# Closing norm of a block of rows run beside the next block's attention: where its squares, roots and row scaling are issued

## What is computed

```
h  = rmsnorm(x) ; proj = h @ w_in -> q, k, v of A, q and latent of B, indexer, two gates
oA = windowed attention (8 heads, sinks, keys of this and the previous chunk)
oB = attention of 8 heads over the 256 keys that the indexer selects per row
x  = x + (sig(gA) * (oA @ wa) + sig(gB) * (oB @ wb)) @ w_out
x  = x + (silu(rmsnorm(x) @ wg) * (rmsnorm(x) @ wu)) @ wd
out = x * rsqrt(mean(x*x) + eps) * g_f          # the norm that the change moves
```

## Time and profile before

| | us |
|---|---|
| median of 3 runs | 3491.55 (3490.05 to 3493.18) |
| profiled execution, its own time | 3493.45 |
| its span, first to last instruction | 3491.6 |
| PE busy | 3371.6 (97%) |
| DVE, ACT, POOL busy | 1931.6, 1392.0, 1639.3 |
| mean granted TensorE clock | 0.99 |

### The profile page before, as it was taken

The page is one execution under the profiler, slowest core; times in us unless marked ns, Lnnn a source line. Parts: engine busy times, 40 slices in busy tenths (PEclk is TensorE's granted clock), DMA queues, the critical chain, the costliest instruction groups (busy, mean ns, idle before and its releaser), DMA issues.

```text
span 3491.6 us, 44043 instructions
## 1 busy us (share of the span) xinstructions
PE 3371.6 (97%) x16616; PEld 2782.9 (80%) x16616; DVE 1931.6 (55%) x3341; ACT 1392.0 (40%) x2547; POOL 1639.3 (47%) x997
## 2 busy tenths in 40 slices
PE   8999999999999999999999998999999999999998
PEld 6778878788887888788788777977887799778887
DVE  3236657468465655376686627767787378521112
ACT  3224435345534431264454226735552377320001
POOL 4555555444235666402566651045667410256665
PEclk9999999999999999999999999999999999999999
DMA  5745454445342333403333351052333500232332
GB/s 143 205 131 169 112 168 127 123 141 157 126 142 93 93 97 97 162 25 129 109 97 91 96 170 37 1 191 83 97 92 97 181 22 2 84 110 91 96 100 93
DMA packets 420642, 382.34 MB, mean 110 GB/s; under 512 B 19248, under 2 KB 347184, under 8 KB 419792
## 3 DMA queue, kind: packets, MB, share of 16 engines
q1 hardware_dynamic: 396512, 337.16, 31.7%
q10 hardware_dynamic: 23920, 42.36, 3.5%
HBM read 316.68 MB, written 62.78 MB: 109 GB/s over the span
## 4 chain that ended last, share of the span: by engine, by line
PE 88%; DVE 5%; ACT 4%; issue 2%; POOL 1%; ACTq 0%; DMA 0%; SPq 0%; DVEq 0%; POOLq 0%
PE BANK L696 20%; PE BANK L697 20%; PE BANK L698 20%; PE BANK L912 3%; PE LP L696 3%; PE LP L697 3%; PE LP L698 3%; PE BANK L925 2%; PE BANK L927 2%; PE LP L889 2%; PE LP L890 2%; PE LP L788 2%; PE LP L787 2%; PE BANK L936 1%; PE LP L895 1%
## 5 line engine op out<-in xcount | busy, mean ns | idle before, releaser
L666 POOL TENSOR_TENSOR WLO<-WRAW,WHI 128x1024 fp32r<-128x1024 f32 x456 | 1118.4, 2453 | 38.0
L664 POOL TENSOR_SCALAR WHI<-WRAW 128x1024 fp32r<-128x1024 f32 x456 | 505.6, 1109 | 1301.9 <-PE BANK L698 954.2
L696 PE MATMUL BANK<-H2hi,WHI 128*128 128x512 f32 x1408 | 560.7, 398 | 6.7 <-DVE X L1780 4.7
L697 PE MATMUL BANK<-H2lo,WHI 128*128 128x512 f32 x1408 | 558.4, 397 | 0.0
L698 PE MATMUL BANK<-H2hi,WLO 128*128 128x512 f32 x1408 | 558.2, 396 | 0.0
L696 PE MATMUL BANK<-HThi,WHI 128*128 128x512 f32 (+1 forms) x1024 | 408.6, 399 | 2.3 <-DVE QS L1428 2.3
L697 PE MATMUL BANK<-HTlo,WHI 128*128 128x512 f32 (+1 forms) x1024 | 404.9, 395 | 0.0
L698 PE MATMUL BANK<-HThi,WLO 128*128 128x512 f32 (+1 forms) x1024 | 404.6, 395 | 0.0
L1192 ACT ACTIVATE MASK<-SCD,THR 128x896 bf16<-128x896 f32 (+5 forms) x186 | 282.0, 1517 | 221.6 <-DVE THR L1487 195.1
L1817 DVE TENSOR_TENSOR BANK<-BANK,SL 128x512 f32<-128x512 f32 x88 | 61.6, 700 | 477.6 <-PE BANK L698 457.8
L696 PEld LDWEIGHTS BANK<-H2hi,WHI 128*128 128x128 f32 x1408 | 265.5, 189 | 72.4 <-DVE X L1780 5.2
(11 more groups left out here) (245 smaller groups left out, 6528.3 us busy)
## 6 DMA issues: line engine op xcount, KB each, us to landing
WRAW<-in_w_in SPq DMA_DIRECT2D x124, 512.0 KB, 4.4
WRAW<-in_w_ffn_gate SPq DMA_DIRECT2D x88, 512.0 KB, 3.9
WRAW<-in_w_ffn_up SPq DMA_DIRECT2D x88, 512.0 KB, 3.8
WRAW<-in_w_ffn_down SPq DMA_DIRECT2D x88, 512.0 KB, 3.8
qsp<-QS SPq DMA_DIRECT2D x32, 512.0 KB, 5.6
gates<-GS ACTq DMA_DIRECT2D x64, 256.0 KB, 2.2
GL<-gates ACTq DMA_DIRECT2D x64, 256.0 KB, 3.7
WRAW<-in_w_out SPq DMA_DIRECT2D x32, 512.0 KB, 4.3
```

What stands on the lines that cost most here:

```text
L664: nc.gpsimd.tensor_scalar(hi, raw, 1.0, 1.0, ALU.mult, ALU.mult).then_inc(w_hi, 1)
L666: nc.gpsimd.tensor_tensor(lo, raw, hi.bitcast(f32), ALU.subtract).then_inc(w_split, 1)
L696: nc.tensor.matmul(dst, whi, mhi, start=first, stop=False)
L697: nc.tensor.matmul(dst, whi, mlo, start=False, stop=False)
```

## The change

ACT's generator runs to i == 0 before it turns to the old block, so the exponentials of pairs 2 and 3 come ahead of it; the second half's squares are then issued one a group, behind the exponentials of groups 0 to 3, and all four roots in group 4. DVE takes one reciprocal of all four columns in group 6 and no longer scales rows, except for the last block. POOL scales the rows: for each tile one instruction with the tile's inverse roots and one with the gains, tiles 0 to 3 in its steps 7 to 10, each behind what that step already had (`whole_sums`, `add_sink`).

```diff
--- before.py
+++ after.py
@@ -226,7 +226,7 @@
         silu_ready, ff_ready, ff_hi, ff_split = (sem(s) for s in ("silu_ready", "ff_ready", "ff_hi", "ff_split"))
         rows_added, rows_squared = sem("rows_added"), sem("rows_squared")
         rows_normed = [sem(f"rows_normed{i}") for i in range(2)]
-        gf_in, y_ready = sem("gf_in"), sem("y_ready")
+        gf_in, y_scaled, y_ready = sem("gf_in"), sem("y_scaled"), sem("y_ready")
         out_done = [sem(f"out_done{j}") for j in range(JT)]
 
         LOW4 = [t[:, h * ROWS:(h + 1) * ROWS] for t in LP for h in range(2)]
@@ -630,6 +630,14 @@
                     nc.gpsimd.tensor_tensor(SN[:, i % 4, :], SINK[:, h0:h0 + 4], MX[:, i % 4, :], ALU.subtract
                                             ).then_inc(sink_ready, made(sink_ready, u))
 
+                def finish_row(j):
+                    pool.wait_ge(gf_in, n(gf_in, b - 1))
+                    pool.wait_ge(rinv_ready, n(rinv_ready, (b - 1, 2, JT - 1)))
+                    nc.gpsimd.tensor_scalar(X1[:, j, :], X1[:, j, :], SS[:, j:j + 1], None, ALU.mult
+                                            ).then_inc(y_scaled, made(y_scaled, (b - 1, j)))
+                    pool.wait_ge(y_scaled, n(y_scaled, (b - 1, j)))
+                    nc.gpsimd.tensor_tensor(X1[:, j, :], X1[:, j, :], GFB[:, :], ALU.mult).then_inc(y_ready, made(y_ready, (b - 1, j)))
+
                 def whole_sums(kind, q):
                     j, hs = q // 2, slice(4 * (q % 2), 4 * (q % 2) + 4)
                     if kind == "b" and len(chunks_of(units(b, "b")[4 * q])) == 1:
@@ -649,6 +657,8 @@
                     for u in range(PAIRS // 2):
                         if i == first_at(b, "a", 2 * u + 1) - 6:
                             add_sink(u)
+                    if b and 0 <= i - 7 < JT:
+                        finish_row(i - 7)
                     if i == first_at(b, "b", 0):
                         split(first_job)
                         split(first_job + 1)
@@ -1081,6 +1091,21 @@
             nc.scalar.copy(WUKhi[:, :], WU[:, 0:2 * HD]).then_inc(wu_hi, 1)
             nc.scalar.copy(WUVhi[:, :], WU[:, 2 * HD:3 * HD]).then_inc(wu_hi, 1)
 
+            def closing(b):
+
+                stage = ("fd", PARTS[-1][0])
+                for j in range(JT):
+                    act.wait_ge(rows_added, n(rows_added, (b, stage, 1, j)))
+                    act.wait_ge(rows_squared, n(rows_squared, (b, stage, 1, j - 1) if j else (b, stage, 0, JT - 1)))
+                    nc.scalar.activation(SQJ[:, :], X1[:, j, ROWS:2 * ROWS], ACT.Square, accum_out=SQB[:, j:j + 1]
+                                         ).then_inc(rows_squared, made(rows_squared, (b, stage, 1, j)))
+                    yield
+                act.wait_ge(var_ready, n(var_ready, (b, 2)))
+                for j in range(JT):
+                    act.wait_ge(rows_squared, n(rows_squared, (b, stage, 1, j)))
+                    nc.scalar.activation(SS[:, j:j + 1], SQB[:, j:j + 1], ACT.Sqrt, bias=SQC[:, j:j + 1], scale=1.0 / D
+                                         ).then_inc(std_ready, made(std_ready, (b, 2, j)))
+
             def attend(b):
 
                 def exps():
@@ -1129,8 +1154,9 @@
                 seq = all_groups(b)
                 probabilities_ = exps()
                 free = 14 if b > 1 else 11
+                rest = closing(b - 1) if b else iter(())
                 for i in range(FIRST, len(seq) + AFTER):
-                    if i == -2:
+                    if i == 0:
                         yield
                     if 0 <= i < len(seq):
                         key = (b,) + seq[i]
@@ -1145,6 +1171,8 @@
                                 out_copy(kind, q // 2)
                     for _ in range(due(exp_times(b), i)):
                         next(probabilities_)
+                    if i >= 0:
+                        next(rest, None)
                     for kind, q in QUADS:
                         if i == quad_end(b, kind, q) + 2:
                             x_copy(kind, q)
@@ -1380,6 +1408,7 @@
                                     pass
                                 ahead[0] = attend(b + 1)
                                 next(ahead[0])
+                                continue
                             for j in range(JT):
                                 square(("fd", part[0]), half, j)
                                 if half:
@@ -1601,6 +1630,7 @@
 
                 seq = all_groups(b)
                 maxima = masks()
+                finished = 6
                 free = 14 if b > 1 else 11
                 for i in range(FIRST, len(seq) + AFTER):
                     if i == -2:
@@ -1611,9 +1641,11 @@
                         dve.wait_ge(pt_hi, n(pt_hi, key))
                         nc.vector.tensor_tensor(PTlo[r][:, 0:w, :], trans(key)[:, 0:w, :], PThi[r][:, 0:w, :].bitcast(f32),
                                                 ALU.subtract).then_inc(pt_ready, made(pt_ready, key))
-                        next(ending[0], None)
                     for _ in range(due(mask_times(b), i)):
                         next(maxima)
+                    if b and i == finished:
+                        dve.wait_ge(std_ready, n(std_ready, (b - 1, 2, JT - 1)))
+                        nc.vector.reciprocal(SS[:, :], SS[:, :]).then_inc(rinv_ready, made(rinv_ready, (b - 1, 2, JT - 1)))
                     for kind, q in QUADS:
                         if i == quad_end(b, kind, q) + 2:
                             invert(kind, q)
@@ -1650,7 +1682,6 @@
                     yield
 
             early = search(0)
-            ending = [iter(())]
 
             def project(b):
                 for k in range(KT):
@@ -1834,19 +1865,13 @@
                             add_row(("fd", part[0]), before, half, len(part) // 2 - 1, j)
                     before = ("fd", part[0])
 
-                def scaled_out(b):
+                if b + 1 == NB:
                     dve.wait_ge(gf_in, n(gf_in, b))
                     for j in range(JT):
-                        dve.wait_ge(std_ready, n(std_ready, (b, 2, j)))
-                        nc.vector.reciprocal(SS[:, j:j + 1], SS[:, j:j + 1]).then_inc(rinv_ready, made(rinv_ready, (b, 2, j)))
+                        inverse(2, j)
                         dve.wait_ge(rinv_ready, n(rinv_ready, (b, 2, j)))
                         nc.vector.scalar_tensor_tensor(X1[:, j, :], X1[:, j, :], SS[:, j:j + 1], GFB[:, :], ALU.mult, ALU.mult
                                                        ).then_inc(y_ready, made(y_ready, (b, j)))
-                        yield
-
-                ending[0] = scaled_out(b)
-            for _ in ending[0]:
-                pass
 
     return C.seen
```

## The result

The changed kernel takes 3504.53 us (median of 7 runs, 3500.85 to 3506.84) against 3491.23 for the kernel before in the same series (7 runs, 3490.05 to 3493.18): a ratio of 1.0036, interval 1.0027 to 1.0046. It is 13 us slower. The prediction said no change, 3489.7 (1.8 us faster), and its range ended at 3498.5: wrong in sign and in range. The profiled execution took 3505.88 us, its span is 3504.1.

A forecast was written before the change was run, and what follows sets the result against it. PE's back-to-back matmuls (88% of the chain) were taken as the bound. Per seam, 4.4 us gained less 2.1 for POOL and 1.7 for the clock left 0.6, 1.8 in three: 3491.55 - 1.8 = 3489.7 us, range 3483.5 to 3498.5.

The forecast's parts named there:

- What bounds the kernel: Whole kernel: PE carries 88% of the chain; the change touches only the seams ahead of attention in blocks 1 to 3.
- steps 1 and 2: Seam start to group 6: exponentials come first, group 0's copy 5.8 us earlier, group 6's copy 4.4 us earlier.
- Step 2: Groups 0 to 5: ACT replaces DVE as bound, with 16.3 us of work; the seam is 4.4 us shorter at group 6.
- Step 3: POOL, groups 10 and 11: tiles of 3.49 us make the second sink 3.1 us late, costing 2.1 us a seam.
- The rival on the other side: POOL's row scaling: scalar instruction by a column takes 2.4 us, a tile 4.83, -3.1 a seam, 3501 us; chance 0.12.
- the slow case: POOL's scaling by a column at 2.4 us makes a tile 4.83 us and the kernel 3501 us; chance 0.12.
- Step 4: Behind POOL's tiles, group 14: DVE's wait for the row writes stays hidden, with 0.1 to 0.8 us to spare.
- Step 5: DVE's port: NM of pairs 14 and 15 held up to 2.4 us by POOL's tile 1, adding nothing.
- Step 6: Clock behind group 11: PE's wait of about 2.3 us lowers it, costing 0 to 3.4 a seam, 1.7 taken.
- The rival with two falls: Clock also falls after PE's wait in groups 1 to 4, costing 1.6 us; -2.7 a seam, 3499.6 us; chance 0.11.
- the sum: Whole kernel: 0.6 us a seam gained, 1.8 us in three, giving 3489.7 us against the median.

The follow-up runs named there:

- old_gains: gains_first with ACT's half undone (squares and roots ahead of the exponentials, as in the kernel before): 3482.37 us, ratio 0.9978 to the kernel before.
- immediate: Changed kernel, but POOL's first instruction of a tile multiplies by constant 1.0 instead of the column of inverse roots: 3489.09 us, ratio 0.999 to the kernel before.
- broadcast: Changed kernel, but POOL scales rows by a two-tensor multiplication with the column repeated over the row: 3497.21 us, ratio 1.0011 to the kernel before.
- gains_first: Changed kernel, but POOL multiplies by the gains in steps 1, 3, 5, 7, DVE by the column in groups 8 to 11: 3483.16 us, ratio 0.9977.
- sink_first: Changed kernel, but POOL's tiles come two steps later, behind the last sinks: 3510.84 us, ratio 1.005 to the kernel before.
- dve_late: Changed kernel, but DVE does both multiplications in one instruction per row, in groups 6 to 9, POOL none: 3489.25 us, ratio 0.9994.

## Why the prediction was wrong

**What bounds the kernel, steps 1 and 2: right.** 5.8 us at group 0 and 4.4 at group 6 were predicted, 5.8 and 4.5 to 4.7 came. The table loads, the squares behind exponentials and the roots behind one load are where it put them. Step 2 names DVE as what bounded these groups before, and ACT's wait of 3.01 us behind DVE's scalings (old_gains) bears it out. That DVE's relief gives nothing beyond ACT's move was right; that it would have given the same by itself (old_gains) was not seen.

**Step 3 failed, by one term.** "The nearest rows are a weight split of the same size in the same stage, which takes 3.49 us": the tile took 5.27. The split scales by two constants, the norm by a column, and at one shape that is 1.05 against 2.85 us. The way from the price to the delay was right, and three kernels with different tiles show it by the same working (distance of the sinks, less the 4.17 of before, less 0.97 absorbed, beside the step measured from group 10 to 11), which comes out 0 to 1.1 us too high:

| kernel | tile us | sinks apart | worked out | measured, blocks 1, 2, 3 |
|---|---|---|---|---|
| immediate | 3.48 | 7.25 | 2.1 | 1.5, 1.6, 2.1 |
| broadcast | 4.33 | 8.92 | 3.8 | 3.0, 3.2, 3.6 |
| changed | 5.27 | 10.83 | 5.7 | 4.6, 5.5, 5.6 |

**The rival on the other side came true, beyond its price.** "POOL's scalar instruction is slow" had 0.12 and an upper bound of 2.4 us, the split's instruction with two tensors. Nothing in the rows made this a bound for a form that they don't show: the multiplication of two tensors by a column takes 1.90, the scalar one 2.85. At 5.27 a tile the prediction's own steps give 4.4 - 5.7 - 1.7 = -3.0 a seam (a loss), and losses of 2.5, 2.8 and 3.0 were measured. With it the forecast would have been 3500.6.

The Trainium skill, page "GPSIMD Engine Reference", section "Engine selection", calls GpSimd roughly line-rate on one input and half as fast as VectorE on two. On 128x1024 the constants fit the first (1.05 us) and the gains the second (2.37 against DVE's 1.23); the column doesn't (2.85 against DVE's 0.75). By that rule the slow case stays away; the trace decides against it here.

**Step 4: right for its tile, wrong for the real one.** 0.1 to 0.8 us were to spare; in immediate the writes stay hidden, after the change DVE waits 1.72 us in block 2 and 1.08 in block 3, and with the tiles two steps later 13.12.

**Step 5: right.** `NM` was to be held by up to 2.4 us at no cost; it took up to 1.38, while ACT waited for the sink anyway. The Trainium skill's rule of the mutual exclusion (page "SBUF — State Buffer", section "Who interferes with whom") agrees with that, and with the 1.31 us of a column scaling in gains_first.

**Step 6: right in kind, and dependent on the wait.** From group 11 to the last one the change loses 1.6, 1.8 and 2.0 us, clock and write wait together, where 1.7 was taken. At the assumed price (immediate) it is 0.0, 0.0 and 1.5. ACT waits 2.5, 2.5 and 3.0 us for the sink there, and the granted clock falls behind group 11 in the last of the three seams alone.

**The rival with two falls: the early one came in every seam of the changed kernel, and its price goes with its place.** Between 2104 and 2112 (block 2) and at the same place in block 3 it costs nothing, group 6 stands at -4.5 and group 10 with it. In block 1 it comes later, 22 to 26 us behind the first addition, and the seam goes from -4.7 to -3.7 between groups 6 and 10. Where it lies from 18 to 26, in one seam each of immediate, broadcast, sink_first and dve_late, 2.0 to 2.1 us are lost over the same groups. The rival had 1.6, the sum nothing. The kernel before has falls in its seams as well, from 8 to 20 us behind the first addition, with the granted clock down to 0.50.

**What stays open.** The seams make 8.3 of the 13.3 us between the medians. For the nine kernels whose seams are given from group 11 to the last (all but sink_first, the repetition counted with the change), the median's difference less that of the profiled seams lies between -1.6 and +5.3 us, 2.4 on the average. Block 0 alone, with the same instructions in each, was 2.1 us shorter to 3.5 us longer than before in single executions, and the four loads of `gates` took 1.78 us in some and about 3 in others. What sets these I did not try to find.

## What to carry to other kernels

Price an operation by its form of operands, not by its size and name: an immediate, a column of scalars and a second tensor were three different prices on one engine. Before work goes to a "free" engine, find its shortest instructions that others wait for, and what lies between two of them. A wait that can be seen (PE's 3.63 us) needn't be what the change must remove: here either of two loads could go, and the better split changed the order of two multiplications, so that the one that needs no root is done early.

## What the hardware showed that I had not expected

GpSimd on 128x1024: scalar instruction with constants 1.05 us, with a column 2.85; two tensors 2.37, but 1.90 where the second is the column repeated. On 128x4 the column form takes 0.30 and two tensors 0.20. The same scaling by a column takes DVE 0.75 us.
